# The first layer's pairs 4 to 6 in three passes, with the derivation of angles and factors in four pieces

## The reference, cut to what matters

```python
for l in range(DEPTH):                         # DEPTH = 2
    mod = (c_act @ w_mod[l] + b_mod[l])[:, None, :]
    sh1, sc1, gt1, sh2, sc2, gt2 = jnp.split(mod, 6, axis=-1)
    h = rmsnorm(x, norm1_g[l]) * (1 + sc1) + sh1
    z = h @ w_cat                              # gates, branch A, branch B, branch C
    ya = rglru_branch(...)                     # factors from lru_lambda
    yb = diff_attention(...)                   # cos/sin of positions, lambda from lq, lk
    yc, v_first = rwkv7_mix(...)               # token shift, low-rank decay / rate / gate
    merged = sigmoid(z_gate_a) * (ya @ w_a) + sigmoid(z_gate_b) * (yb @ w_b) + sigmoid(z_gate_c) * (yc @ w_c)
    x = x + gt1 * (merged @ w_out[l])
    x = x + gt2 * conv_gated_mlp(rmsnorm(x, norm2_g[l]) * (1 + sc2) + sh2, ...)

ang = positions[..., None] * inv_freq          # the angles; cos(ang), sin(ang) rotate q and k
lam = exp(sum(lq1 * lk1)) - exp(sum(lq2 * lk2)) + lambda_init
log_a = -8 * r * softplus(-lru_lambda)
```

## Time and profile before

| | before |
|---|---|
| median of 3 runs | 1118.03 us |
| lowest, highest | 1117.86 us, 1120.5 us |
| the profiled execution, its own time | 1121.91 us |
| its span, first to last instruction | 1120.1 us |
| PE busy | 1097.3 us (98% of the span) |
| DVE busy | 839.3 us (75%) |
| ACT busy | 586.0 us (52%) |
| mean granted TensorE clock | 0.994 |

### The profile page before, as it was taken

One profiled execution on the slowest core, in us unless ns is written; L12 is line 12 of the kernel. 1 busy time (PEld: TensorE's weight loads), 2 busy tenths in 40 slices (PEclk: granted clock), 3 DMA queues, 4 the chain that ended last, 5 costly groups with the idle time before them and its releaser, 6 DMA issues.

```text
span 1120.1 us, 24386 instructions
## 1 busy us (share of the span) xinstructions
PE 1097.3 (98%) x10190; PEld 1007.1 (90%) x10190; DVE 839.3 (75%) x1245; ACT 586.0 (52%) x897; POOL 125.7 (11%) x142
## 2 busy tenths in 40 slices
PE   8999999999999999999999999999999999999997
PEld 7889987888789999999989999777887999999996
DVE  4798998765487898987768899966636868888763
ACT  2266577522274666663445565762226566666533
POOL 0100000156002000001110000013530100000001
PEclk8999999999999999999999999999999999999999
DMA  9945555443146466768835555471614455555651
GB/s 378 334 164 222 179 193 202 152 170 136 77 150 264 164 236 226 242 222 305 317 128 197 185 187 194 153 260 40 220 47 155 177 195 188 187 187 187 215 199 38
DMA packets 41464, 214.88 MB, mean 192 GB/s; under 512 B 7936, under 2 KB 8320, under 8 KB 22048
## 3 DMA queue, kind: packets, MB, share of 16 engines
q1 hardware_dynamic: 29856, 171.65, 42.0%
q0 software_dynamic: 11520, 41.95, 10.8%
HBM read 212.01 MB, written 1.05 MB: 190 GB/s over the span
## 4 chain that ended last, share of the span: by engine, by line
PE 94%; DVE 2%; ACT 2%; issue 1%; DMA 0%; DVEq 0%; ACTq 0%
PE ps L1769 17%; PE ps L1767 17%; PE ps L1768 17%; PE ps L1956 6%; PE ps L1958 6%; PE ps L1962 5%; PE ps L1787 5%; PE ps L2067 5%; PE ps L1728 2%; PE ps L2242 1%; PE ps L2058 1%; PE ps L1752 1%; PE ps L1746 1%; PE ps L1983 1%; PE ps L1913 1%
## 5 line engine op out<-in xcount | busy, mean ns | idle before, releaser
L962 ACT ACTIVATE WH<-ring 128x1024 fp32r<-128x1024 f32 x144 | 151.9, 1060 | 166.9 <-PE ps L1769 157.7
L1628 DVE TENSOR_TENSOR WLO<-ring,WH 128x1024 fp32r<-128x1024 f32 x144 | 175.5, 1231 | 72.6 <-ACT WH L962 72.6
L1769 PE MATMUL ps<-HH,WLO 128*128 128x256 f32 x736 | 208.1, 283 | 0.0
L1768 PE MATMUL ps<-HL,WH 128*128 128x256 f32 x736 | 206.7, 281 | 0.0
L1767 PE MATMUL ps<-HH,WH 128*128 128x256 f32 x736 | 205.0, 279 | 0.0
L1769 PEld LDWEIGHTS ps<-HH,WLO 128*128 128x128 f32 x736 | 138.7, 188 | 0.0
L1767 PEld LDWEIGHTS ps<-HH,WH 128*128 128x128 f32 x736 | 138.5, 188 | 0.0
L1768 PEld LDWEIGHTS ps<-HL,WH 128*128 128x128 f32 x736 | 138.0, 188 | 0.0
L560 POOL DMA_DIRECT2D mring<-wmod_dram x80 | 43.2, 540 | 771.3 <-DVE macc L1112 452.9
L1769 PE MATMUL ps<-GH,WLO 128*128 128x256 f32 x384 | 108.3, 282 | 0.0
L1767 PE MATMUL ps<-GH,WH 128*128 128x256 f32 x384 | 108.2, 282 | 0.0
(11 more groups left out here) (402 smaller groups left out, 2599.1 us busy)
## 6 DMA issues: line engine op xcount, KB each, us to landing
ring<-wmain_dram SPq DMA_DIRECT2D x150, 1024.0 KB, 4.9
mring<-wmod_dram POOLq DMA_DIRECT2D x80, 512.0 KB, 5.1
G<-wmod_dram SPq DMA_DIRECT2D x3, 1024.0 KB, 9.7
R<-wmod_dram SPq DMA_DIRECT2D x3, 1024.0 KB, 17.6
TK<-wmod_dram SPq DMA_DIRECT2D x2, 1024.0 KB, 20.8
X<-x_t_dram SPq DMA_DIRECT2D x1, 1024.0 KB, 5.5
y_dram<-H SPq DMA_DIRECT2D x4, 256.0 KB, 2.2
SW<-small_dram SPq DMA_DIRECT2D x1, 512.0 KB, 13.7
```

What stands on the lines that cost most here:

```text
L962: A(WH[:, n % 2, part], ring[:, b, part], ACT.Copy).then_inc(hi_ready, 1)
L1628: V.tensor_tensor(WLO[:, n % 2, part], ring[:, b, part], WH[:, n % 2, part].bitcast(F32), ALU.subtract).then_inc(lo_ready, 1)
L1768: MM(out, w_high[:, at], low, start=False, stop=False, skip_group_check=True)
L1769: return MM(out, w_low[:, at], high, start=False, stop=stop, skip_group_check=True)
```

## The change

In the first layer pairs 4, 5 and 6 go from `product` to `product_split`, and what that needs is put where it is needed. `split_from(0)` becomes 4. `input_high` moves ahead of the low-rank tanh on ACT, `input_low` moves ahead of kk on DVE, and the helpers `next_high` and `early_low` now work in the first layer too. The low-rank weights go into `R` (tiles 8 to 11), since `HG0` is written over `SW` earlier, and their load is issued after that of pair 4. `derived()` is cut: its first part with the angles and the first reduction stands before the wait for PE's shift column; the second reduction (`reduced(1, ...)`) stands after the low parts of pair 10, the factors (`derived_last()`) after those of pair 7, the signing of the sine after those of pair 13. ACT's two sines move behind the roots of kk, ahead of the reading of pair 9.

```diff
         def split_from(l):
-            return 1 if l else LR
+            return 1 if l else 4
+        def halves_before(l):
+            return 2 * (GA - split_from(0)) * l
...
-                if l == 0:
-                    sp.dma_start(lora_weights(l, WL, 1024), small[l, :, 0:1024]).then_inc(s_sw, 16)
...
                 for k in range(4, UP + 4):
                     pair(PAIRS * l + k)
+                    if (l, k) == (0, 4):
+                        sp.wait_ge(mod_used, added(FIRST - 1))
+                        sp.dma_start(lora_weights(WL, 1024), small[l, :, 0:1024]).then_inc(s_sw, 16)
...
                 def next_high(k):
-                    if l:
+                    if k + 2 >= split_from(l):
                         half_pairs_high(2 * (k + 2 - LR), 2 * (k + 3 - LR))
...
                 evac(l, 2, G[:, 4:6, :])
+                if l == 0:
+                    input_high()
                 next_high(2)
                 act.wait_ge(lora_z, 2 * l + 2)
...
                     A(sm[:, 48:56], sm[:, 40:48], ACT.Ln, bias=sm[:, ONE1:ONE1 + 1]).then_inc(pre_act, 1)
-                    act.wait_ge(pre_dve, 5)
-                    A(SIN[:, :], RT[:, :], ACT.Sin).then_inc(pre_act, 1)
-                    A(COS[:, :], YB[:, 1, :], ACT.Sin).then_inc(pre_act, 1)
...
-                if l == 0:
-                    input_high()
-                    half_pairs_high(0, 4)
-                else:
-                    next_high(5)
+                next_high(5)
                 evac(l, 6, G[:, 12:14, :])
+                next_high(6)
...
                     A(E[:, 2 * b:2 * b + 2, :], E[:, 2 * b:2 * b + 2, :], ACT.Exp, scale=-0.5).then_inc(kk_rt, 1)
+                if l == 0:
+                    act.wait_ge(pre_dve, 5)
+                    A(SIN[:, :], RT[:, :], ACT.Sin).then_inc(pre_act, 1)
+                    A(COS[:, :], YB[:, 1, :], ACT.Sin).then_inc(pre_act, 1)
...
+                    derived()
                     dve.wait_ge(cw_mm, 1)
                     V.tensor_copy(sm[:, CSH:CSH + 4], ps[:, 5, 0:4]).then_inc(cw_ready, 1)
...
                 def early_low(k):
-                    if l:
+                    if k >= split_from(l):
                         half_pairs_low(2 * (k - LR), 2 * (k + 1 - LR))
...
                 early_low(3)
-                if l == 0:
-                    derived()
...
                 early_low(4)
+                if l == 0:
+                    input_low()
...
                 early_low(7)
+                if l == 0:
+                    derived_last()
...
                 if l == 0:
-                    half_pairs_low(0, 2)
-                    input_low()
                     half_pairs_low(2, 4)
...
                 half_pairs_low(7, 8)
+                if l == 0:
+                    reduced(1, YB[:, 1, :])
                 dve.wait_ge(kk_rt, 2 * (l + 1))
...
                 half_pairs_low(12, 14)
+                if l == 0:
+                    dve.wait_ge(pre_act, 6)
+                    V.tensor_scalar(SIN[:, :], SIN[:, :], sm[:, CSH:CSH + 1], None, ALU.mult).then_inc(step, tick(n_step))
+                    after()
...
                 for k in (4, 5):
-                    if l:
-                        product_split(l, k)
-                    else:
-                        product(l, k, H)
+                    product_split(l, k)
...
+                product_split(l, 6)
                 if l:
-                    product_split(l, 6)
                     product_split(l, LR)
...
                 else:
-                    product(l, 6, H)
                     product_split(l, LR)
                     product_split(l, LR + 1)
```

More of the change, by code:

```diff
@@ L354, in split_from, with lora_weights @@
         def split_from(l):
-            return 1 if l else LR
-        def lora_weights(l, a, n):
-            return (R[:, 8:12, :].rearrange("p a b -> p (a b)") if l else SW)[:, a:a + n]
+            return 1 if l else 4
+        def halves_before(l):
+            return 2 * (GA - split_from(0)) * l
+        def lora_weights(a, n):
+            return R[:, 8:12, :].rearrange("p a b -> p (a b)")[:, a:a + n]
         def half_high(y):
@@ L688, in half_pairs_high @@
                         if far and m == 0:
-                            act.wait_ge(p_half, (GA - LR) * l + k - 2 - split_from(l) + 1)
+                            act.wait_ge(p_half, halves_before(l) // 2 + k - 2 - split_from(l) + 1)
                         elif far:
@@ L1052, in derived @@
                 V.tensor_scalar(ang, YB[:, 1, :], C[:, FREQ:FREQ + 1], None, ALU.mult).then_inc(step, tick(n_step))
[L1053 to L1069, removed]
@@ new lines, in derived, with reduced @@
+                reduced(0, red)
+            def reduced(n, out):
+                ang, k1 = YB[:, 2, :], YB[:, 3, :]
+                after()
+                V.tensor_scalar(k1, ang, 1.0 / SQ2PI, 0.25 * n, ALU.mult, ALU.add).then_inc(step, tick(n_step))
+                after()
+                V.tensor_scalar(k1, k1, MAGIC, None, ALU.add).then_inc(step, tick(n_step))
+                after()
+                V.tensor_scalar(k1, k1, -MAGIC, None, ALU.add).then_inc(step, tick(n_step))
+                after()
+                V.scalar_tensor_tensor(out, k1, -C1, ang, ALU.mult, ALU.add).then_inc(step, tick(n_step))
+                after()
+                V.scalar_tensor_tensor(out, k1, -C2, out, ALU.mult, ALU.add).then_inc(step, tick(n_step))
+                after()
+                V.scalar_tensor_tensor(out, k1, -C3, out, ALU.mult, ALU.add).then_inc(step, tick(n_step))
+                after()
+                V.tensor_scalar(out, out, 0.5 * math.pi * n, PI_IN, ALU.add, ALU.min).then_inc(step, tick(n_step))
+                after()
+                V.tensor_scalar(out, out, -PI_IN, None, ALU.max).then_inc(pre_dve, 1)
@@ L1070, in derived, with derived_last @@
+            def derived_last():
                 dve.wait_ge(pre_act, 4)
@@ L1088, in derived @@
                 after()
-                V.reduce_sum(sm[:, 24:25], mat(ROT), AX_X).then_inc(step, tick(n_step))
+                V.reduce_sum(sm[:, CSH:CSH + 1], mat(ROT), AX_X).then_inc(step, tick(n_step))
                 after()
-                V.tensor_scalar(sm[:, 24:25], sm[:, 24:25], -1.0, None, ALU.mult).then_inc(step, tick(n_step))
-                after()
-                dve.wait_ge(pre_act, 6)
-                V.tensor_scalar(SIN[:, :], SIN[:, :], sm[:, 24:25], None, ALU.mult).then_inc(step, tick(n_step))
-                after()
+                V.tensor_scalar(sm[:, CSH:CSH + 1], sm[:, CSH:CSH + 1], -1.0, None, ALU.mult).then_inc(step, tick(n_step))
             def mod_block(n):
@@ L1858, in _ @@
                     for j in range(4):
-                        last = MM(duo(4 + 2 * i + j // 2)[:, j % 2, :], lora_weights(l, WL + j * P, P)[rows, :], YA[rows, 0, :],
+                        last = MM(duo(4 + 2 * i + j // 2)[:, j % 2, :], lora_weights(WL + j * P, P)[rows, :], YA[rows, 0, :],
                                   start=True, stop=True)
@@ L1862, in _ @@
                 for k in (4, 5):
-                    if l:
-                        product_split(l, k)
-                    else:
-                        product(l, k, H)
+                    product_split(l, k)
                 pe.wait_ge(lora_act, 10 * l + 4)
                 for j in range(4):
-                    last = MM(duo(4 + j // 2)[:, j % 2, :], lora_weights(l, WG + j * P, P), YA[:, 1, :], start=True, stop=True)
+                    last = MM(duo(4 + j // 2)[:, j % 2, :], lora_weights(WG + j * P, P), YA[:, 1, :], start=True, stop=True)
                 last.then_inc(lora_mm, 1)
+                product_split(l, 6)
                 if l:
-                    product_split(l, 6)
                     product_split(l, LR)
```

8 lines of the change are left out of this document (3 added, 5 removed).

## The result

Measured together in 15 executions each, the changed kernel took 1123.09 us (median; 1118.77 to 1131.22) and the kernel before 1120.17 us (1116.36 to 1122.65). The ratio is 1.0038, 95% interval 1.0021 to 1.0054: 4.2 us slower, 2.4 to 6.0; the medians differ by 2.9 us only, since a few executions of the changed kernel are long (four of the 15 lie above 1127). A second comparison of the same two kernels, 12 executions against 35, gave 1.0049 (1.0027 to 1.0071). The forecast was 1.2 to 1.3 us slower, with a range up to 1122.4. The direction was as forecast; the loss was more than twice the forecast, and the time lies 0.7 us above the range.

A forecast was written before the change was run, and what follows sets the result against it. PE was taken as the bound (94% of the span), with DVE nearly full at 47 to 143 us. Saved 3.95, stalls 5.15, net +1.2, plus 0.1, on the median 1118.03 gave 1119.3 us; range 1115.6 to 1122.4.

The forecast's parts named there:

- PE's saving: Pairs 4 to 6 on PE: each converted pair saves about 1.32 us, three save 3.95, all on the chain.
- DVE's added work, the copy and the tanh: At 47 to 62 us: shift column's copy 2.5 late, tanh behind four activations, PE's low-rank products stall 2.3 us.
- The small weights: Low-rank weights loaded behind pair 4: landing at 54 to 55 us, covered by the stall; at 61.6 adding 2.3.
- rival C: Loads come late: small weights land at 61.6, PE's first stall is 4.6; 1120 to 1121.5 us; chance 0.11.
- Pairs 8, 11 and 14: PE waits there for late low parts: stalls of 0.45, 1.6 and about 0.8 us.
- the sum: Over the changed stretch: saved 3.95, stalls 5.15, net +1.2 us; 0.1 added for what follows pair 16.
- The signs of being wrong: Low-rank products starting by 57.5 us, gates before 142.8, or granted clock under 1 at 56 to 66 us.
- The third sign: A granted clock under 1 at 56 to 66 us would show the forecast wrong.
- The table load: On ACT, ahead of pair 9's reading: one more load of 1.28 us, without the skill's drain of 1.38 us.
- rival B: Clock falls at PE's 2.3 us stall: half speed some 6.5 us, about 3.3 us lost, 1122.6 us; chance 0.07.

The follow-up runs named there:

- the tanh first: The changed kernel with ACT's low-rank tanh ahead of the rounding of the input and of pair 4's high parts: 1119.77 us, ratio 1.0005.
- the longer wait: The changed kernel with two unused activations on ACT ahead of the low-rank tanh: 1125.56 us, ratio 1.0069.
- the part put back: The changed kernel with the first part of the derivation back behind the two modulation blocks: 1127.36 us, ratio 1.0071.
- the third single execution of the changed kernel: The changed kernel, nothing altered, traced a third time to see where the granted clock falls: 1124.02 us.
- the run at 176 us: The changed kernel with the low-rank tanh first on ACT and two modulation blocks moved from between pairs 9 and 10 to 176 us: 1118.99 us, ratio 0.9999.
- the blocks at 188 us: The changed kernel with the low-rank tanh first on ACT and two modulation blocks moved from between pairs 9 and 10 to 188 us: 1127.48 us, ratio 1.0062.

## Why the prediction was wrong

**PE's saving (3.95 us).** Nearly right. From the start of the low-rank products to pair 7's end the kernel before takes 31.27 us and the changed one 27.54, a saving of 3.7. By the pieces of the chain pair 4 takes 5.84 us where pair 7, in the same first-pair form, took 5.66 before; the low-rank products took 2.94 and not 2.90.

**DVE's added work, the copy and the tanh.** Right. The first part lies between the shift column and the copy, from 47.07 to 51.81 us, the tanh came behind four roundings, and the stall is 2.35 us against 2.3 forecast.

**The small weights.** Right in its likely case: with the tanh first PE had them by 56.31 us without a wait, and rival C didn't come.

**Pairs 8, 11 and 14.** Right in place; sizes 0.61, 1.56 and 0.39 on the timeline against 0.45, 1.6 and 0.8. Measured from one pair's start to another's, where the wait inside a matmul's recorded length counts too, they are 0.8, 1.8 and 0.7. With the smaller saving this makes 87.67 - 85.71 = 1.96 us to the gates, where the sum had 1.2. The terms of the sum that were mis-sized are pair 8 (0.35 short), pair 11 (0.2 short), pair 14 (0.15 too much) and the saving (0.25 too much). Behind the gates the sum had 0.1 us. The traces show 0.4 us there (972.5 against 972.1), and all executions together 2.9 us for the whole span, so the order alone cost more than twice the forecast.

**The signs of being wrong.** Two of the three came up in the profiled execution: the low-rank products started at 56.22 us, ahead of 57.5, and the gates at 141.6, ahead of 142.8. Neither says what it was meant to say, since the late early fall shifted both. The signs should have been lengths from pair 3's end. The third sign, a clock under 1 at 56 to 66 us, came in one of the five traces.

**The table load.** The rows were right: 1.28 us and no drain. The drain that the Trainium skill adds (ScalarE: Activation LUTs, What ACT_TABLE_LOAD costs) is in none of these traces, before or after: where the activation behind a load waits for no other engine it starts 0.02 us later.

**The steps that failed.** Two did, each with about 1.7 us more than the forecast held. The first is the sum: the order costs 2.9 us in span less clock loss and not 1.3, of which the stretch to the gates explains 2.0 by the terms above. The second is the clock (rival B), which the sum held at nothing. The mechanism stood there, with a chance of 0.07, as an all-or-nothing case of 3.3 us. The runs show it as something that happens in a part of the executions: a mean clock of 0.990 or less in 7 of 27, against 1 of 87. In the mean it is 1.8 us of clock loss, a term of the sum and not a rival to it. The one traced execution with the fall behind the stall lost 4.7 us to the gates by it, but 1.8 to 3.3 counted from the span's start; its mean clock is 0.992, and none of the 7 was traced, so where their clock fell is not shown. The prediction said itself that the stall was longer than any in the trace after the start; it gave no reason for a chance of 0.07, and no row of the trace before could give one. It was also wrong that the clock was at full speed for the rest of the span: the same trace has 3.4 us of half clock at 744 to 749 us and more at its end, so falls were commoner than it took them for.

The Trainium skill (TensorE: Matmul & The Clock Gate, Why this matters for your kernels) warns of idle gaps between bursts, and the traces of the longer wait, of the part put back and of the third single execution of the changed kernel agree with it, each with half clock at or right behind the idle time. That the stall matters is supported by the two runs that took it away in different ways (the tanh first, the unused matmuls): 0 of 24 executions at 0.990 or less, and 0 of 12 in the run at 176 us, which has the tanh first too. If the stall made no difference, 0 of 24 beside 7 of 27 would come up about once in 130 times. Against it stands the longer wait, with 1 of 7 and hardly more clock loss; so half clock behind a stall of 2.3 or 4.2 us comes in some executions only, and what decides it stays open.

**The sum in the end.** 2.0 us in order and 1.8 in clock make 3.8 of the 4.2 us. That is less settled than it looks: in executions whose early fall comes late the order costs only 0.25 us, so the mean over executions is under 2.0; and span less clock loss differs by 2.9 us over all executions. The stretch behind the gates, less clock loss, has means of 972.5 and 972.1 us with a scatter of 1 us. So about 1 us has no place of its own. A part may be which executions were traced: the five of the kernel before average 1111.2 us less clock loss, against 1110.4 over all 87, while the five of the changed kernel (1113.1) stand where all 27 do. Or the half-clock stretches delay DVE's releases beyond their own length; no run tested either, and it stays open.

**The baseline.** The kernel before had 1118.03 us in the three executions shown and 1120.17 in fifteen. Its executions lie between 1114.5 and 1124.2 us, longer with more half-clock stretches, so a forecast against three of them had 1 to 2 us of error from this alone. Against 1120.17 the same sum gives 1121.4 us, 1.7 under the measured time: that the time lay outside the range owes something to the baseline, that the loss was mis-sized does not. The range also ended at 1122.4 us, under rival B's own 1122.6.

## What to carry to other kernels

Where DVE is at 19 of 20 us, fewer passes on PE bought nothing here: follow DVE's list and count which of its holes the new work can really fill. A wait of PE that looks cheap can have a second price, the clock, which is paid in some executions only; read the clock of many executions, not of one profile. Taking the tanh first, which left half of the stall, gained 3.8 us in the means here; filling the stall with unused matmuls gained 2.1 (0.4 in the medians). Work that is moved out of a full stretch must land where its buffer has been refilled, or the wait comes back there: 4.36 us for the blocks at 188 us, while at 176 us that wait was gone and a smaller one of 1.4 us came.

## What the hardware showed

The same changed kernel had its first half-clock stretch at 21 to 28 us in two of five traces, at 38 to 43 us in two and behind the stall at 56 us in one. With the one at 38 to 43 us the first stall was 0.66 and 0.67 us, in the other three 2.34 to 2.39. But for that at a trace's end, the half-clock stretches last 3.4, 6.8 or 10.2 us. Between pair 3's end and the gates the kernel before repeats to 0.03 us over five executions, while the spans of the same five differ by 4 us. Part of that is the clock; behind the gates they still differ by 2.9 us with the clock loss taken off.
